# A two-layer diffusion trunk on one core: cached keys and time constants loaded later, and grouped units that begin with the products of high parts

## What is computed

```python
h = rms(x) * (1 + sc1) + sh1                 # sc, sh, g come from silu(cond) @ w_ada
gates, xa, qkv_da, xc, mla_in = split(h @ w_in)
out_a = pool_mixer(xa)                       # windowed means of 2, 4, 8, 16 tokens, divided by the count
out_b = diff_attention(q1, q2, k, v)         # latent tokens also see cached keys and values
out_c = fourier(xc)                          # 2-D Fourier transform by products with cosine and sine matrices
out_d = mla_attention(rms(c_q) @ w_uq, rms(c_kv) @ w_ukv, cached ckv and krope)
merged = sum(sigmoid(gates) * (branches @ w_branch))
x = x + g1 * (merged @ w_out)
h2 = rms(x) * (1 + sc2) + sh2
x = x + g2 * conv_ffn(h2)                    # w_up, width-3 convolution, silu, w_down
```

## Time and profile before

| | us |
|---|---|
| median of 3 runs | 1248.19 |
| lowest, highest | 1247.5, 1248.64 |
| the profiled execution, its own time | 1250.48 |
| span of its trace | 1248.7 |
| TensorE busy (of the span) | 1235.4 (99%) |
| VectorE busy | 790.9 (63%) |
| ScalarE busy | 575.1 (46%) |
| GpSimd busy | 130.2 (10%) |

### The profile page before, as it was taken

One profiled execution on the slowest core, in us unless ns is written; L12 is line 12 of the kernel. 1 busy time (PEld: TensorE's weight loads), 2 busy tenths in 40 slices (PEclk: granted clock), 3 DMA queues, 4 the chain that ended last, 5 costly groups with the idle time before them and its releaser, 6 DMA issues.

```text
span 1248.7 us, 20286 instructions
## 1 busy us (share of the span) xinstructions
PE 1235.4 (99%) x8200; PEld 1159.1 (93%) x8200; DVE 790.9 (63%) x1484; ACT 575.1 (46%) x949; POOL 130.2 (10%) x109
## 2 busy tenths in 40 slices
PE   7999999999999999999999999999999999999999
PEld 6977999889989999999989879998899999999998
DVE  5545576548778777773363656764495978777532
ACT  3435565533365444442244446645334655455321
POOL 0212000006400000000014200000092000000000
PEclk9999999999999999999999999999999999999999
DMA  9852233553733444448543312345446234343443
GB/s 371 308 198 87 80 107 123 189 193 105 267 135 123 154 159 161 148 154 285 190 184 136 129 68 95 104 147 178 154 165 240 102 119 135 119 135 119 135 143 127
DMA packets 52685, 195.68 MB, mean 157 GB/s; under 512 B 6320, under 2 KB 6736, under 8 KB 51440
## 3 DMA queue, kind: packets, MB, share of 16 engines
q1 hardware_dynamic: 52272, 193.69, 44.7%
q0 software_dynamic: 320, 0.69, 0.2%
HBM read 192.10 MB, written 2.26 MB: 156 GB/s over the span
## 4 chain that ended last, share of the span: by engine, by line
PE 94%; DVE 2%; DMA 2%; issue 1%; ACT 0%; SPq 0%; DVEq 0%
PE bank L1330 27%; PE bank L1332 26%; PE bank L1331 26%; PE bank L1289 2%; PE bank L1632 1%; PE bank L1612 1%; DMA start_ada<-start_ada 1%; DVE w_lo L912 1%; PE bank L1398 1%; PE bank L1402 1%; PE bank L1602 1%; PE bank L1403 1%; DMA ada<-ada_w 1%; PE bank L1587 1%; PE bank L1387 1%
## 5 line engine op out<-in xcount | busy, mean ns | idle before, releaser
L1330 PE MATMUL bank<-act_hi,w_hi 128*128 128x384 f32 x1368 | 465.9, 341 | 1.1 <-DVE act_lo L956 0.7
L1332 PE MATMUL bank<-act_hi,w_lo 128*128 128x384 f32 x1368 | 457.8, 335 | 0.0
L1331 PE MATMUL bank<-act_lo,w_hi 128*128 128x384 f32 x1336 | 446.8, 334 | 0.0
L912 DVE TENSOR_TENSOR w_lo<-w_raw,w_hi 128x1024 fp32r<-128x1024 f32 x251 | 314.5, 1255 | 188.7 <-ACT w_hi L599 188.2
L599 ACT ACTIVATE w_hi<-w_raw 128x1024 fp32r<-128x1024 f32 x251 | 264.2, 1053 | 160.8 <-DMA w_raw<-stream 160.6
L1330 PEld LDWEIGHTS bank<-act_hi,w_hi 128*128 128x128 f32 x1368 | 257.3, 188 | 13.6 <-issue 9.6
L1332 PEld LDWEIGHTS bank<-act_hi,w_lo 128*128 128x128 f32 x1368 | 256.9, 188 | 0.0
L1331 PEld LDWEIGHTS bank<-act_lo,w_hi 128*128 128x128 f32 x1336 | 251.1, 188 | 0.6
L1330 PE MATMUL bank<-mlp_hi,w_hi 128*128 128x384 f32 x352 | 118.7, 337 | 0.0
L1332 PE MATMUL bank<-mlp_hi,w_lo 128*128 128x384 f32 x352 | 118.3, 336 | 0.0
L1331 PE MATMUL bank<-mlp_lo,w_hi 128*128 128x384 f32 x352 | 118.3, 336 | 0.0
(11 more groups left out here) (235 smaller groups left out, 1530.5 us busy)
## 6 DMA issues: line engine op xcount, KB each, us to landing
w_raw<-stream SPq DMA_DIRECT2D x251, 512.0 KB, 3.3
ada<-ada_w SPq DMA_DIRECT2D x56, 512.0 KB, 4.3
start_ada<-start_ada SPq DMA_DIRECT2D x8, 1024.0 KB, 18.1
ada_norm<-ada_w SPq DMA_DIRECT2D x16, 512.0 KB, 5.6
ada_head_a<-ada_w SPq DMA_DIRECT2D x8, 512.0 KB, 5.4
start_raw<-start_w SPq DMA_DIRECT2D x8, 448.0 KB, 18.7
params<-params SPq DMA_DIRECT2D x2, 926.0 KB, 12.4
x<-x_in SPq DMA_DIRECT2D x2, 768.0 KB, 5.4
```

The costliest lines, as they stand in the source:

```text
L912: V.tensor_tensor(wlo[s][:, :], raw[s][:, :], whi[s][:, :].bitcast(F32), ALU.subtract).then_inc(lo_ready, 1)
L1330: T.matmul(out, wb[s][0][:, w, :], hi[k], start=first and k == 0, stop=False)
L1331: T.matmul(out, wb[s][0][:, w, :], lo[k], start=False, stop=False)
L1332: ins = T.matmul(out, wb[s][1][:, w, :], hi[k], start=False, stop=last and k == n - 1)
```

## The change

The loads of `cached` and `time_consts` leave the head of each layer and are issued behind the load that waits for the last mixer unit (number 12); `cached` gets a semaphore of its own, for which VectorE waits ahead of L1067 and TensorE ahead of L1504. The first unit waits for `unit_done` at that place in SyncE's queue go with the load.

In `group` the matmuls of a block are regrouped: first high by high of all units that take part in the block, which waits for the high part of the activation only, then high activation by low weight of all, and then, after the wait for the low part, low activation by high weight of all.

```diff
-                sp.dma_start(ca[:, :], caches[l:l + 1, :, :].rearrange("a p n -> (a p) n")).then_inc(par_loaded, 16)
...
-                if l == 0:
-                    sp.wait_ge(unit_done, FROM + SKIP)
-                sp.dma_start(tc[:, :], time_consts).then_inc(tc_loaded, 16)
                 first_step = G0 + PREP_GATES
                 for u in range(SLOTS if l else SKIP + SLOTS, first_step + SLOTS):
                     load_unit(u)
+                    if u - SLOTS == U_MIX - 1:
+                        sp.dma_start(ca[:, :], caches[l:l + 1, :, :].rearrange("a p n -> (a p) n")).then_inc(ca_loaded, 16)
+                        sp.dma_start(tc[:, :], time_consts).then_inc(tc_loaded, 16)
...
-                    dve.wait_ge(par_loaded, 32 * l + 32)
+                    dve.wait_ge(par_loaded, 16 * l + 16)
...
+                dve.wait_ge(ca_loaded, 16 * (l + 1))
                 src = ca[NOPE:QKW, HC - PAST:HC].unsqueeze(1).to_broadcast([ROPE, HEADS, PAST])
...
-                def group(u, banks, hi, lo, wait, lag=0):
+                def group(u, banks, hi, lo, wait_hi, wait_lo, lag=0):
...
+                    parts = [wb[(l * UNITS + u + q - SKIP) % SLOTS] for q in range(3)]
                     for k in range(KD):
-                        wait(k)
-                        for q in range(2):
-                            if k == 0:
+                        at = k - lag
+                        now = [(q, k) for q in range(2)] + ([(2, at)] if 0 <= at < half else [])
+                        wait_hi(k)
+                        for q, c in now:
+                            if c == 0:
                                 unit_ready(u + q)
-                            ins = dense(outs[q], u + q, [k], hi[k:k + 1], lo[k:k + 1], k == 0, k == KD - 1)
-                            if k == KD - 1:
+                            T.matmul(outs[q], parts[q][0][:, c, :], hi[c], start=c == 0, stop=False)
+                        for q, c in now:
+                            T.matmul(outs[q], parts[q][1][:, c, :], hi[c], start=False, stop=False)
+                        wait_lo(k)
+                        for q, c in now:
+                            ins = T.matmul(outs[q], parts[q][0][:, c, :], lo[c], start=False, stop=q < 2 and c == KD - 1)
+                            if q < 2 and c == KD - 1:
                                 ins.then_inc(unit_done, 1)
-                        at = k - lag
-                        if 0 <= at < half:
-                            if at == 0:
-                                unit_ready(u + 2)
-                            dense(outs[2], u + 2, [at], hi[at:at + 1], lo[at:at + 1], at == 0, False)
...
+                pe.wait_ge(ca_loaded, 16 * (l + 1))
                 for h in range(HEADS):
                     ins = T.matmul(bank[2][half(h), h // 2 * PAST:(h // 2 + 1) * PAST], wk[:, h, 0:NOPE], ca[:, 512:512 + PAST],
```

More of the change, by code:

```diff
@@ L345, in program @@
                            "par_loaded"))
+        ca_loaded = sem("cached_loaded")
         tc_loaded, stored, y_stored = sem("tc_loaded"), sem("stored"), sem("y_stored")
@@ L1418, in _ @@
                     hole_units()
-                    group(0, (0, 1, 2), HI, LO, lambda k: pe.wait_ge(norm_lo, l * 2 * KD + k + 1))
+                    group(0, (0, 1, 2), HI, LO, lambda k: pe.wait_ge(norm_hi, l * 2 * KD + k + 1),
+                          lambda k: pe.wait_ge(norm_lo, l * 2 * KD + k + 1))
                 def values(u):
@@ L1697, in _ @@
                 pe.wait_ge(gated_ready, FROM + (l + 1) * KD * 4 - 4)
-                group(O0, OUT_BANK[0:3], MH, ML, lambda k: pe.wait_ge(mrg_lo, l * KD + k + 1), lag=2)
+                group(O0, OUT_BANK[0:3], MH, ML, lambda k: pe.wait_ge(mrg_hi, l * KD + k + 1),
+                      lambda k: pe.wait_ge(mrg_lo, l * KD + k + 1), lag=2)
                 pe.wait_ge(gated_ready, FROM + (l + 1) * KD * 4)
@@ L1706, in _ @@
                 norm_units(l)
-                group(P0, (0, 1, 2), HI, LO, lambda k: pe.wait_ge(norm_lo, (l * 2 + 1) * KD + k + 1))
+                group(P0, (0, 1, 2), HI, LO, lambda k: pe.wait_ge(norm_hi, (l * 2 + 1) * KD + k + 1),
+                      lambda k: pe.wait_ge(norm_lo, (l * 2 + 1) * KD + k + 1))
                 for j in range(3, SLOTS):
```

## The result

The changed kernel takes 1250.41 us in the median of 22 runs (1249.63 to 1252.78), the kernel before 1248.47 us in 22 runs of its own (1247.5 to 1251.81): a ratio of 1.0016, 95% interval [1.001, 1.0022]. That is 1.9 us, 0.16%, slower, and inside the 0.2% that I had called no change. The interval lies above 1, so the loss is real, but it is under the 2.5 us that the likeliest case of the prediction wanted. The forecast was 1251.5 us, in a range of 1248.7 to 1253.7. The profiled execution of the changed kernel took 1252.78 us, with a span of 1251.0, against 1250.48 and 1248.7 before.

A forecast was written before the change was run, and what follows sets the result against it. TensorE, busy 1235.4 of 1248.7 us, was taken to bound the kernel, so only its gaps count. Terms -0.42 + 0 + 1.62 + 2.1 = +3.3 us on 1248.19 gave 1251.5 us, range 1248.7 to 1253.7.

The forecast's parts named there:

- the likeliest case of the prediction: Whole kernel: slower as worked out, by a sum over 2.5 us; chance 0.48.
- Groups at `O0`: O stage, both layers: more matmuls left behind the waits for weight splits, 0.69 plus 0.12 us at `O0+3`; +1.62 in all.
- Groups at `P0`: P stage, both layers: earlier start given back at `P0+4`, behind a VectorE chain without slack; 0 in each layer.
- the group starts 0.59 us earlier: At `P0`: TensorE, free at 354.70, starts on the high part instead of idling 0.59 us for the low part.
- Unit 0 of layer 1: Group there: start 0.77 us earlier, less 0.35 as unit 0 ends two matmuls later in block 7; -0.42 at unit 3.
- The moved loads: Latent norms: late `time_consts` makes GpSimd's window products collide with VectorE's three norms; 0.4 and 1.7 us, +2.1 in all.
- by its fastest landing of 5.7 us: Landing of `time_consts` behind unit 16's load: at 93.5 and 710.3, or half a microsecond earlier, 93.0 and 709.8.
- The sum: All terms: -0.42 + 0 + 1.62 + 2.1 = +3.3 us, giving a median of 1251.5 us.
- Norms not hit: Rival at the latent norms: load misses them or engines don't exclude each other; sum +1.2, 1249.4 us; missed or grazed, chance 0.32.
- A new stall that halves the clock: Rival: a stall of 1.7 us at 714 lowers TensorE's clock; sum +5.0, 1253.2 us; chance 0.09.
- Stall at 74 gone: Rival in layer 0: 1091 KB less queued removes the modulation load stall, 3.9 us in all; chance 0.06.
- Start gains kept: Rival: earlier starts (0.59 twice, 0.77) stay and regrouping costs nothing at `O0`; -1.95, with norms hit 1248.3 us; chance 0.05.

The follow-up runs named there:

- e5: Changed kernel, with the low part of the weights waited for only ahead of the products that read it: 1249.74 us against 1248.13, ratio 1.0013.
- e6: Changed kernel, with unit `P0+4` split ahead of the tanh for the first pair of the P stage: 1250.67 us against 1248.13, ratio 1.002.
- e8: Kernel before, with high parts first only at unit 0 of layer 1 and `P0`, block 7 in old order, plus edits of e6 and e7: 1247.23 us, ratio 0.9988.
- e9: As e8, with the pair of modulation loads issued ahead of unit 12's load too: 1249.51 us against 1248.04, ratio 1.001.
- e1: Kernel before, with only the two loads moved and the group as it was: 1249.82 us against 1248.44, ratio 1.0009.
- e7: Changed kernel, with the pair of modulation weight loads issued ahead of unit 13's load: 1249.36 us against 1248.13, ratio 1.0008.
- e3: Changed kernel, with GpSimd's window products made to wait for the latent norm of their layer: 1250.53 us against 1248.44, ratio 1.0015.
- e12: Kernel before, with the load of `cached` alone moved and `time_consts` where it was: 1248.14 us against 1248.04, ratio 1.0000.
- e10: Changed kernel, with both moved loads one unit earlier, behind unit 15's load: 1250.61 us against 1248.04, ratio 1.002.
- e11: Changed kernel again, unchanged, for a second trace: 1250.55 us against 1248.04, ratio 1.002.

## Why the prediction was right, and where it wasn't

**Groups at `O0`: right.** +0.81 per layer forecast, +0.76 and +0.76 measured. Idles of about 0.6 and 0.75 were forecast, and 0.60 and 0.77 found. At `O0+3` 0.12 us of stall were forecast, and its first weight load stands 0.28 us behind the last one, 0.11 more than usual (329.64 and 329.92). e5 shows the mechanism.

**Groups at `P0`: right in the sum, wrong in the first step.** The step "the group starts 0.59 us earlier" failed: it starts 0.18 us earlier. I took TensorE to be free at 354.70, at the end of its last load; 0.41 us of issue stand behind a modulation step also where the profile shows no wait. The chain on VectorE took all of the rest, as forecast, and e6, e8 and e9 show that it does: with the split moved, 0.26 to 0.31 us stay, but for layer 1 of e6, where a load was late. So the zero was right, and the 0.75 us of idle that I had forecast at `P0+4` were 0.35.

**Unit 0 of layer 1: the number right, one of its reasons by luck.** -0.42 forecast, -0.39 measured, and the start came 0.75 us earlier where I had 0.77. But that the lost 0.35 us hung on the order of block 7 was not borne out by e8: with the old order there, the low part of block 7 held TensorE for 0.34 us, nearly the same.

**The moved loads: the mechanism right, the term mis-sized in both layers.** I took +0.4 in layer 0 and +1.7 in layer 1; it was +1.34 and +0.24 in the profiled execution. The step is "by its fastest landing of 5.7 us", less half a microsecond for a queue that already runs. The landings were 7.1 and 6.8 us from the issue, nearer the median of 7.7 that stood beside the 5.7, so the load landed over a microsecond later than I had it, in the middle of the bad window in layer 0 and behind the first norm in layer 1. The queue that already ran didn't make it shorter. (The load that took 5.7 us was issued at 52.8, behind the last of the seven starting units; the text ahead of the prediction says the first.) So in layer 1 the first norm kept its 0.62 us, which the prediction had named as a sign that it is wrong, and only the two behind it were hit. That the two misses, +0.9 and -1.5 us, go opposite ways is luck: it leaves 1.6 us beside the 2.1 forecast. In layer 0 the price depends on the execution. Where the products began 0.27 to 0.48 us ahead of the first norm, as in e1, e5 and e7, the stretch lost 0.36 to 0.55; where they began 0.68 to 0.87 ahead, as in e6 and both traces of the changed kernel, 1.19 to 1.39, with one more product in front of the third norm. e3 shows that the collision is all of it, e12 that `cached` has no part in it, e10 that the rotary step of VectorE is hit as well. The Trainium skill (SBUF — State Buffer, "Who interferes with whom") has the two engines exclude each other where VectorE reads two inputs from SBUF and GpSimd reads too; the traces agree, with norms of 0.61 us alone in e3 and 1.09 to 1.66 us beside a product in the changed kernel, and with the rotary sum of e10.

**The sum.** +3.3 forecast for the body, +2.68 and +2.52 in the two traces. In medians it was +1.9 here and +2.5 beside e11. The two bodies agree within 0.2 us; what the head adds to a median is not settled. No trace shows that the changed kernel's head is earlier, and none excludes it.

**The rivals.** Norms not hit: false. A new stall that halves the clock: false, no stall at the norms was over 1.43 us and the clock stayed whole there. Stall at 74 gone: false, it is in both kernels, and its length differs from execution to execution (first idle of 1.30 and 0.76 us in the two traces of the changed kernel). Start gains kept: false, but for 0.39 us in layer 1.

## What to carry to other kernels

A load that is moved later moves its first reader too, also when that reader sits on an engine that nobody waits for: look for every consumer. Where it is GpSimd that reads, look also for what VectorE does at that time with two inputs in SBUF. In a group of units, wait for each part only ahead of the products that read it; an order that puts more work behind a wait and less ahead of it loses what stands behind. Where medians of two versions differ by less than the spread of one, compare the stretches between landmarks of their traces: here they repeated within 0.05 us, while the head, with its late loads, moved by 5.

## What the runs showed of the hardware

A product of GpSimd that meets VectorE doesn't get every second turn. In layer 1 the last pair of products took 6.27 us, against 1.98 for a pair alone, beside three splits of VectorE back to back that took 3.48, no more than 1.16 each. The first of the two, of 256 columns, takes 0.74 us alone; here it took 4.33 and ended at 719.65, 0.59 us behind the last split. GpSimd stood behind all three. In the layer 0 rows, with other work between the norms, each waited for the other.

A modulation load of 512 KB can land at different times with the same issues ahead of it. In the two traces of the changed kernel the first of the pair was issued at 67.37 and 67.22, and released TensorE at 73.74 and 73.04: 6.37 and 5.82 us. In e7 and e8 it was issued at 67.0 in both, with the same issues in the ten microseconds ahead, and was there by 72.3 in one and at 73.53 in the other.
